# RWKV block doubling: one copy of Y and one block transpose for both heads of a tile

## The reference, cut to what matters

```python
def step(S, inp):
    r_t, w_t, kk_t, a_t, k_t, v_t = inp
    sa = jnp.einsum('bhvk,bhk->bhv', S, -kk_t)
    S = (S * w_t[:, :, None, :] + sa[..., None] * (kk_t * a_t)[:, :, None, :]
         + v_t[..., None] * k_t[:, :, None, :])
    return S, jnp.einsum('bhvk,bhk->bhv', S, r_t)
```

## Time and profile before

| what | value |
|---|---|
| median of 3 runs | 3253.72 us (3253.22 to 3254.35) |
| the profiled execution's own time | 3258.47 us |
| its span | 3256.9 us |
| mean granted TensorE clock | 0.878 |
| PE / DVE / ACT / POOL busy | 92% / 36% / 18% / 5% |
| STREAM_TRANSPOSE L1711 | 160 times, 345 ns each |
| Y copies L1309 of 160 columns | 160 times, 304 ns each |

### The profile page before, as it was taken

How to read it: one execution, slowest core, us unless ns; L and a number is a source line. 1 busy time by engine, 2 the same in 40 slices (tenths; PEclk the granted TensorE clock), 3 DMA queues, 4 the chain that set the end, 5 groups by cost and what they waited for, 6 DMA issues and landing times.

```text
span 3256.9 us, 56498 instructions
## 1 busy us (share of the span) xinstructions
PE 2994.0 (92%) x25136; PEld 1844.5 (57%) x25136; DVE 1166.6 (36%) x1906; ACT 599.6 (18%) x1118; POOL 157.5 (5%) x192
## 2 busy tenths in 40 slices
PE   7999988888888889999999999889888888999998
PEld 2555754665656565555525557446666565655554
DVE  4243546526252531111142544554262626211110
ACT  2111133213131210000021111432121313110000
POOL 0010000010000010000000100000001010000000
PEclk9999999768686868999999999996776868699999
DMA  6211100000000001111151111000000000011111
GB/s 241 80 42 58 59 26 26 22 3 28 3 28 3 27 4 40 58 65 58 59 200 52 50 58 60 19 33 15 12 19 9 22 3 28 3 52 59 65 58 58
DMA packets 38271, 147.08 MB, mean 45 GB/s; under 512 B 4720, under 2 KB 4720, under 8 KB 37136
## 3 DMA queue, kind: packets, MB, share of 16 engines
q1 hardware_dynamic: 34704, 128.47, 11.8%
q0 software_dynamic: 3328, 15.02, 1.2%
HBM read 139.27 MB, written 4.19 MB: 44 GB/s over the span
## 4 chain that ended last, share of the span: by engine, by line
PE 83%; DVE 10%; issue 3%; ACT 2%; DMA 1%; POOL 0%; DVEq 0%; POOLq 0%; another core or an unknown queue 0%; ACTq 0%
PE ps L463 81%; DVE scr L1750 1%; DVE scr L1574 1%; PE ps L828 1%; DVE scr L1596 1%; DVE scr L1587 1%; DVE scr L1743 1%; DVE scr L1711 1%; DVE scr L1586 0%; DVE scr L1755 0%; ACT scr L1295 0%; PE ps L719 0%; DVE scr L1746 0%; ACT scr L1296 0%; DMA par<-in_par 0%
## 5 line engine op out<-in xcount | busy, mean ns | idle before, releaser
L463 PE MATMUL ps<-h,ring 128*128 128x512 f32 (+1 forms) x4480 | 1244.4, 438 | 3.2 <-issue 3.2
L463 PE MATMUL ps<-scr 32*32 32x32 f32 (+11 forms) x17320 | 962.5, 258 | 164.8 <-issue 53.7
L463 PEld LDWEIGHTS ps<-h,ring 128*128 128x128 f32 x4480 | 691.9, 193 | 557.1 <-issue 555.3
L463 PEld LDWEIGHTS ps<-scr 32*32 32x32 f32 (+5 forms) x17320 | 692.0, 147 | 416.6 <-issue 211.7
L1798 DVE SCALAR_TENSOR_TENSOR scr<-scr,ps 128x640 f32<-128x640 f32 x48 | 39.4, 821 | 508.5 <-PE ps L463 508.0
L463 PE MATMUL ps<-scr,cst 128*128 128x512 f32 (+2 forms) x480 | 137.9, 410 | 9.6 <-ACT scr L1273 9.6
L463 PE MATMUL ps<-scr,ring 128*128 128x512 f32 (+1 forms) x512 | 140.7, 438 | 4.0 <-DVEq L1803 4.0
L1342 ACT ACTIVATE scr<-ps 128x640 f32<-128x640 f32 x48 | 33.8, 704 | 563.7 <-PE ps L463 563.7
L1766 DVE COPY scr<-ps 128x128 f32<-128x128 f32 x80 | 23.3, 292 | 267.5 <-PE ps L463 264.8
L463 PEld LDWEIGHTS ps<-scr,ring 128*128 128x128 f32 x512 | 78.2, 193 | 66.5 <-issue 66.5
L1309 ACT ACTIVATE scr<-ps 128x160 f32<-128x160 f32 x192 | 62.5, 325 | 279.3 <-PE ps L463 278.0
(11 more groups left out here) (244 smaller groups left out, 2210.4 us busy)
## 6 DMA issues: line engine op xcount, KB each, us to landing
ring<-in_w SPq DMA_DIRECT2D x240, 512.0 KB, 3.3
x<-in_x SPq DMA_DIRECT2D x1, 2560.0 KB, 16.0
yc<-in_win POOLq DMA_DIRECT2D x2, 1280.0 KB, 7.8
out_y<-x POOLq DMA_DIRECT2D x1, 2560.0 KB, 7.7
scr<-in_inv POOLq DMA_DIRECT2D x2, 1152.0 KB, 5.3
scr<-in_tab POOLq DMA_DIRECT2D x4, 512.0 KB, 8.9
cst<-in_cst POOLq DMA_DIRECT2D x1, 1466.0 KB, 9.3
scr<-in_ck POOLq DMA_DIRECT2D x2, 256.0 KB, 3.3
```

Source lines behind the costliest of these rows:

```text
L463: return nc.tensor.matmul(out, lhsT, rhs, start=start, stop=stop)
```

## The change

The Y copies of levels 0 to 4 serve both heads in one ACT instruction of 2 x 160 columns, from the two neighbouring PSUM banks; it waits until y of both heads is done. The block transposes serve both heads in one DVE instruction of 320 columns, after the masked copies of both heads (and, at the start, after the first multiply and add of both). TensorE's code is unchanged: both heads' semaphore counts now rise at once. The Y copies of level 5 stay as they were.

```diff
+                        def y_of_both_out(lev):
+                            act.wait_ge(Y_full, 12 * g + 2 * lev + 2)
+                            A_(t3(Yc, NT * 32), t3(ps[:, 3072:4096], 512)[:, :, 0:NT * 32], ACT.Copy).then_inc(Y_ready, 2)
+
                         for lev in range(4):
-                            for hh in range(2):
-                                y_out(Yc, lev, hh)
+                            y_of_both_out(lev)
                             if lev in (1, 2):
                                 product_out(ABQ[lev - 1], lev - 1, lev)
                             if d == 0 and lev >= 2:
                                 decay(g + 1, lev - 2)
-                        for hh in range(2):
-                            y_out(Yc, 4, hh)
+                        y_of_both_out(4)
...
-                        def turned(hh):
-                            dve.sem_inc(TT_ready, 1)
-                            V.transpose(of_head(Tc, hh), of_head(TTc, hh)).then_inc(T_ready, 1)
+                        def turned():
+                            dve.sem_inc(TT_ready, 2)
+                            V.transpose(Tc, TTc).then_inc(T_ready, 2)
...
                             link(TTn(tt, t3(of_head(Ac, hh), 32), over_units(f"first{d}"), MUL))
                             link(TTn(tt, tt, over_units("ident32"), ADD))
-                            turned(hh)
+                        turned()
...
                                                        halves32(block_bank(hh)[:, 0:NT * 32], b, 1 - d)))
-                                turned(hh)
+                            turned()
```

## The result

The changed kernel takes 3297.3 us (median of 4 runs, 3278.5 to 3304.0) against 3254.0 us before: a ratio of 1.0122, 95% interval 1.0078 to 1.0166. A second set of 5 runs gave 3285.5 us (3283.7 to 3294.1) against 3253.8: 1.0101, interval 1.0087 to 1.0114. So it is slower by 32 to 43 us, about 1%. I had forecast slower by 14 us, 3268, with a range of 3256 to 3286. The sign was right; the size was off by a factor of two to three.

What follows compares the result with a forecast made beforehand. TensorE, busy 92%, was taken as the bound, with code-packet stalls absorbing shorter delays. 16 x (0.2 + 0.1 + 0.45), 2 x 0.8 and 6 x 0.1 gave +14 us on 3253.7: 3268 us, range 3256 to 3286.

Steps and rivals of the forecast that it cites:

- The prices: Durations of the two new instructions: common transpose of 320 columns 0.51 us, common copy of 2 x 160 columns 0.43 us.
- Point 5, level 4: Joined(0) waits for the common copy, +0.45 us a group; the transpose before level 4 is nearly hidden, +0.1 us.
- Point 2, the copy at levels 0, 1 and 3: A product between y(1) and joined(0) covers the longer common copy at these levels: just hidden, no cost.
- Point 1, the start: Start of a group: earlier multiply, longer transpose and y(0) now ahead of y(1) sum to +0.2 us a group.
- the clock: Rival: denser matmul runs raise TensorE's clock, 3249 us, 7% faster; 5% for a slow side beyond the forecast.
- code packets follow from there: Start of a group: later code packets shift with the +0.2 us there, so that delay carries through.
- Point 4, level 2: Levels 1 to 2: 1.1 to 1.5 us absorbed in 14 groups (six odd ones +0.1); groups 0 and 8 lose 0.8 each.
- Absorbed, just: Level 2, group 3: delay of 1.1 to 1.5 us fits some 1.5 us of room, including a 1.31 us stall.
- every level pays: Rival, 15%: stalls for code move with TensorE instead of absorbing delays; total +35 us, 3289 us.
- Point 3, the transposes after levels 0, 2 and 3: Products between joined(1) and the next y(0) hide the longer common transpose, nearly so after level 0: nothing lost.

Runs made afterwards that it cites:

- copy_only: The kernel before with the common Y copies of levels 0 to 4 and the old per-head transposes; 6 us slower than before by the medians.
- copy_l03: The kernel before with the common Y copy at levels 0 to 3 only; these copies cost nothing in time.
- transpose_only: The kernel before with the common transposes and the old per-head copies; the transposes cost 27 us.
- fill1_start: The changed kernel with one extra unused matmul of 256 columns ahead of y(0) of level 0; ratio 1.0082 to the kernel before.
- start_split: The changed kernel with the first transposes of each group per head again; 3275.3 us.
- best: The changed kernel with transposes per head at group start and after level 1, and level 4 copies per head; 15 us slower than before.
- two_split: The changed kernel with the transposes per head again at the start of a group and after level 1; 3278.5 us.
- wait_l2: The kernel before with y(0) of level 2 also waiting for head 1's transpose; 3 us slower (interval 0 to 5.5).

## Why the prediction was wrong, point by point

*The prices* of the instructions: right, 511 and 437 ns against 510 and 430.

*Point 5, level 4:* right for the copy, low for what comes ahead of it. Forecast +0.45 and 0.1 us a group; D4 grew by 0.41, Y4 by 0.24. copy_only against copy_l03 measures the copy alone at 7 us, as in the sum.

*Point 2, the copy at levels 0, 1 and 3:* right, and more: copy_l03 shows it free at level 2 as well.

*Point 1, the start:* failed, and is the largest error. I priced it at +0.2 us a group, 3 us in all. It measured +1.23 with level 0, 20 us. The waits themselves were priced right: 0.23 to 0.25 us wherever the clock stays full and no stall comes (transpose_only, fill1_start). The sum has no term for the clock, and that is what failed: in most groups TensorE falls to half clock behind the hole of 1.33 us, and takes 4.23 us for what takes 3.05 at full clock behind the same hole. By the windows of fill1_start this is 11 to 13 us of the 20. What the waits and the clock leave, some 4 us, lies mostly in odd groups, where at full clock too a stall of 1.3 to 1.5 us can open inside level 0; "code packets follow from there" was too simple. I had named the clock, but as a rival that would make the kernel faster, and gave 5% to the other side with no price. The rows for it were there: the clock of 0.64 to 0.76 in the earlier trace rows and 0.85 against 0.4 us for 20 matmuls at either level. What I didn't do was to ask at which place the clock was still full, and whether my change put a hole just ahead of it.

*Point 4, level 2:* failed in the odd groups. "Absorbed, just" was read from the 1.31 us of stall in the earlier trace rows, with the stall's end taken as fixed. It isn't: a packet begins only after TensorE gets past a place in the code before it. A wait ahead of that place moves the packet, and the stall starts again behind it (1.09 us at 859.63). The reading was too generous besides: in the view of the earlier trace rows the stalls behind y(1) of level 2 in the eight odd groups are 0.96 to 1.51 us, and only two of them reach the 1.3 us that I gave to all. I had this very argument in the rival "every level pays" and set it aside because the packets came evenly. They come evenly when code is the limit, and 5 to 6 us apart as soon as a wait is. In six of the even groups, where the stall lay behind the boundary, level 2 did absorb: 0.20 us in start_split against 1.14 in the odd ones. Groups 0 and 8, forecast at 0.8 each, lost 1.68 and 0.70 there. So absorption is real, but it depends on which side of the boundary the wait stands.

*Point 3, the transposes after levels 0, 2 and 3:* "nothing" held for the pieces just behind them (Y1 +0.08, Y3 -0.15 us). But best, which keeps these, is 15 us slower than before, and in its even groups the packets run late from level 3 on and joined(0) of level 4 stands still for 0.3 to 0.9 us. I followed each delay to the next stall only, and not to the packets behind it.

*The rest.* Forecast were 14 us over the windows, 0.9 a group; measured were 40.8, 2.55 a group. Of the difference the clock at the start is 11 to 13 us by the windows of fill1_start, level 2 some 10 us by the windows, which the measured time of two_split did not confirm. With all three places undone 15 us remain. Part of it is the stall at level 4 of the even groups; the other parts stay open.

*The range* of 3256 to 3286 was built from the prices and the rivals one at a time. The clock and the late code came together.

## What to carry to other kernels

Joining two instructions that serve two independent streams into one saves work where there was idle time, and takes away the overlap that the two streams gave each other. Before you count a hole on TensorE at its length, look at the granted clock just behind it: here waiting for both heads cost 0.2 us by itself, and the hole of 1.3 us that it made cost another 1.2 us by the clock behind it, in most groups but not in all. And a stall for code is a cushion only for a wait that stands behind the place that sets off the next packet; a delay ahead of it goes on to the packets that follow.

## What the runs showed of the hardware

- TensorE's code comes in packets of 16 KB, in group 3 of the kernel before one in 3.3 to 3.9 us; the shortest distance anywhere in the traces of before and after is 3.0 us. A packet begins only after TensorE has got past a place in the code before it: in wait_l2, start_split and the changed kernel the distance grows to 5 or 6 us when a semaphore holds TensorE there, and the same packet begins at the same instruction (14.7 to 17.2 us into group 5 in five kernels). The Trainium skill (Runtime: NRT & Kernel Launch, section Instruction fetch mechanics) says that the fetch is hidden; here, if the "issue" pieces are this fetch as rows and packets suggest, it stood open for 25.1 us over seven groups before.
- One matmul of 256 columns that computes nothing, in a hole of 1.33 us, raised the mean granted clock 3 to 6 us into the groups from 0.62 (0.71 in the second profile) to 0.98.
- The kernel before repeats within 12 us over all sets (3249 to 3261), the changed one within 26 (3278 to 3304). The clock at the start of its groups falls one way or the other from group to group, in the same code.
- A copy of 2 x 160 columns from two neighbouring PSUM banks takes 437 ns, one of 320 in one access of half the partitions 432.
